# Idle products at norm ends, high halves first in the first units, and a convolution term on ScalarE in an 18-stage block stack

## The reference

```
h = rmsnorm(x, pre_g)
x = x + 0.5 * rmsnorm((silu(h @ w_gate) * (h @ w_up)) @ w_down, post_g)   # feed-forward, RMS
x = x + rmsnorm(mixer(rmsnorm(x, pre_g)), post_g)                          # mixer, RMS
x = layer_norm(ALPHA * x + f(x), g, b)                                     # the four LayerNorm stages
causal_dwconv(u, w, b): out[t] = b + sum over r in 0..3 of w[r] * u[t - 3 + r]   # per channel, 2048 channels
```

## Time and profile before

| what | us |
|---|---|
| median of 3 runs (lowest, highest) | 3450.58 (3449.51, 3451.14) |
| the profiled execution's own time | 3452.58 |
| its span, first to last instruction | 3450.8 |
| TensorE busy | 3232.1 (94%) |
| VectorE busy | 1790.2 (52%) |
| ScalarE busy | 1507.1 (44%) |
| GpSimd busy | 909.6 (26%) |
| mean granted clock of TensorE | 0.941 |

### The profile page before, as it was taken

One profiled execution on the slowest core, in us unless ns is written; L12 is line 12 of the kernel. 1 busy time (PEld: TensorE's weight loads), 2 busy tenths in 40 slices (PEclk: granted clock), 3 DMA queues, 4 the chain that ended last, 5 costly groups with the idle time before them and its releaser, 6 DMA issues.

```text
span 3450.8 us, 63449 instructions
## 1 busy us (share of the span) xinstructions
PE 3232.1 (94%) x27080; PEld 3094.7 (90%) x27080; DVE 1790.2 (52%) x3034; ACT 1507.1 (44%) x2512; POOL 909.6 (26%) x486
## 2 busy tenths in 40 slices
PE   8998999998797999988988999999899999999998
PEld 8997999996687999988977899999889999986998
DVE  5446555547664545347575444454535436445543
ACT  5444444543323444446554544344424435443442
POOL 3221232322343332322211223232213222221222
PEclk9988999998898999999998999999899999997899
DMA  6542354554101554533432435455323544540353
GB/s 228 187 160 74 129 186 163 187 174 153 68 3 50 196 186 166 186 135 117 152 116 98 147 129 186 139 172 177 102 78 131 175 168 144 169 143 25 127 173 116
DMA packets 133384, 484.49 MB, mean 140 GB/s; under 512 B 14959, under 2 KB 17151, under 8 KB 132399
## 3 DMA queue, kind: packets, MB, share of 16 engines
q1 hardware_dynamic: 131120, 470.25, 39.9%
q0 software_dynamic: 1984, 10.19, 0.9%
HBM read 479.34 MB, written 1.05 MB: 139 GB/s over the span
## 4 chain that ended last, share of the span: by engine, by line
PE 83%; DVE 8%; ACT 4%; issue 3%; POOL 1%; DMA 0%; SPq 0%; DVEq 0%; POOLq 0%; ACTq 0%
PE ps L182 82%; ACT hi L179 1%; ACT arena L179 1%; DVE lo L159 1%; PE ps L190 1%; DVE tmp L167 1%; DVE arena L159 1%; DVE arena L167 1%; DVE yT L167 1%; ACT L179 1%; POOL small L159 1%; DVE small L176 0%; DVE tmp L164 0%; DVE xT L159 0%; POOL arena L159 0%
## 5 line engine op out<-in xcount | busy, mean ns | idle before, releaser
L182 PE MATMUL ps<-hh,lo 128*128 128x256 f32 (+1 forms) x4624 | 1335.3, 289 | 0.0
L182 PE MATMUL ps<-hh,hi 128*128 128x256 f32 (+1 forms) x4336 | 1264.8, 292 | 60.0 <-DVE hl L167 26.8
L182 PE MATMUL ps<-hl,hi 128*128 128x256 f32 (+1 forms) x4336 | 1253.4, 289 | 0.0
L159 POOL TENSOR_TENSOR lo<-raw,hi 128x1024 fp32r<-128x1024 f32 x271 | 688.6, 2541 | 1827.9 <-ACT hi L179 1827.8
L179 ACT ACTIVATE hi<-raw 128x1024 fp32r<-128x1024 f32 x814 | 852.1, 1051 | 446.4 <-PE ps L182 339.7
L159 DVE TENSOR_TENSOR lo<-raw,hi 128x1024 fp32r<-128x1024 f32 x543 | 696.0, 1285 | 551.2 <-ACT hi L179 530.5
L182 PEld LDWEIGHTS ps<-hh,hi 128*128 128x128 f32 x4336 | 842.8, 194 | 73.5 <-DVE hl L167 29.5
L182 PEld LDWEIGHTS ps<-hh,lo 128*128 128x128 f32 x4624 | 896.6, 194 | 0.0
L182 PEld LDWEIGHTS ps<-hl,hi 128*128 128x128 f32 x4336 | 840.7, 194 | 0.2
L182 PE MATMUL ps<-hfh,lo 128*128 128x256 f32 (+1 forms) x1760 | 499.1, 284 | 0.0
L182 PE MATMUL ps<-hfh,hi 128*128 128x256 f32 (+1 forms) x1520 | 430.8, 283 | 0.0
(11 more groups left out here) (363 smaller groups left out, 3766.0 us busy)
## 6 DMA issues: line engine op xcount, KB each, us to landing
raw<-in_l_ffn_w_gate SPq DMA_DIRECT2D x88, 512.0 KB, 3.6
raw<-in_l_ffn_w_up SPq DMA_DIRECT2D x88, 512.0 KB, 3.7
raw<-in_l_ffn_w_down SPq DMA_DIRECT2D x88, 512.0 KB, 3.3
raw<-in_g SPq DMA_DIRECT2D x88, 512.0 KB, 3.2
raw<-in_u SPq DMA_DIRECT2D x88, 512.0 KB, 3.2
raw<-in_d SPq DMA_DIRECT2D x88, 512.0 KB, 3.2
raw<-in_ffn_w_gate SPq DMA_DIRECT2D x44, 512.0 KB, 3.2
raw<-in_ffn_w_up SPq DMA_DIRECT2D x44, 512.0 KB, 3.3
```

The source lines that it names most:

```text
L159: return self.e.tensor_tensor(o, a, b, op)
L182: return self.e.matmul(o, a, b, start=first, stop=final, skip_group_check=loose)
```

## The change

A method `hold(pe, bank, n)` issues n products of the constant identity with itself, 128 by 128 by 128, into bank 3, whose content nobody reads. They are put into TensorE's list at the three kinds of norm ends, in front of its waits. The first units of four mixers and of the feed-forward blocks (but for the first block and the one behind `Shared`) run, for each tile, the eight products with its high part after `hh(k)`, and the four with its low part after `hl(k)`. In the convolution ScalarE makes tmp = w3 * u + b out of the bank, with scale and bias from the parameter columns, ahead of its copy; VectorE is left with three steps, and only the last two wait for VectorE's own.

```diff
+    def hold(self, pe, bank, n):
+        for _ in range(n):
+            pe.mm(self.ps[bank][:, 0:P], self.ident, self.ident)
...
     def pe(self, pe):                                   # RmsExit
-        self.norm.sums(pe, [(4, self.pr(2)), (6, self.ysq(6)), (7, self.ysq(7))], False, True)
+        K, more = self.K, self.T == T3
+        self.norm.sums(pe, [(4, self.pr(2))], False, False)
+        K.hold(pe, 3, 1)
+        self.norm.sums(pe, [(6, self.ysq(6)), (7, self.ysq(7))], False, True)
+        K.hold(pe, 3, 6 if more else 4)
         self.norm.spread(pe)
+        K.hold(pe, 3, 5)
...
     def pe(self, pe):                                   # LayerExit
+        K = self.K
         self.means(pe)
-        self.norm.sums(pe, self.squares())
+        K.hold(pe, 3, 7)
+        for part, first, final, n in ((0, True, False, 2), (1, False, False, 2), (2, False, False, 1), (3, False, False, 0),
+                                      (4, False, True, 4)):
+            self.norm.sums(pe, self.squares()[part:part + 1], first, final)
+            K.hold(pe, 3, n)
         self.norm.spread(pe)
+        K.hold(pe, 3, 6)
...
     def pe(self, pe):                                   # Full
-        self.norm.sums(pe, [(k, self.sq(k)) for k in range(8)])
+        for k in range(8):
+            self.norm.sums(pe, [(k, self.sq(k))], k == 0, k == 7)
+            self.K.hold(pe, 3, 4 if k == 7 else 2 if self.T == T1 else 1)
         self.norm.spread(pe)
+        self.K.hold(pe, 3, 4)
...
+    def firsts(self, pe, u, banks):                     # Ffn; Mixer.first is changed to the same order
+        K, T = self.K, self.T
+        for k in range(8):
+            pe.wait_ge(*self.entry.hh(k))
+            for i, bank in enumerate(banks):
+                K.W.need(pe, u + i)
+                hi, lo = K.W.col(u + i, k)
+                pe.mm(bank[:, 0:T], hi, K.H[:, k, 0:T], k == 0, False)
+                pe.mm(bank[:, 0:T], lo, K.H[:, k, 0:T], False, False)
+            pe.wait_ge(*self.entry.hl(k))
+            for i, bank in enumerate(banks):
+                t = pe.mm(bank[:, 0:T], K.W.col(u + i, k)[0], K.L[:, k, 0:T], False, k == 7)
+                if k == 7:
+                    t.then_inc(K.W.done, 1)
...
                         if j > 3:                       # Hybrid.act
                             act.wait_ge(*self.cv(j - 4))
+                        act.act(K.tmp[:, j % 4, 0:T1], p, ACT.Identity, scale=K.col("conv_w_2", 48 + j),
+                                bias=K.col("conv_b_2", j))
                         t = act.act(self.uu[:, j % 4, 3:259], p, ACT.Copy)
...
-        wc = [K.col("conv_w_2", r * 16 + j) for r in range(4)]      # Hybrid.conv
-        if j > 3:
-            dve.wait_ge(*self.sx(j - 4))
-        dve.mark(dve.ts(v, u[:, 3:259], wc[3], K.col("conv_b_2", j), ALU.mult, ALU.add))
+        wc = [K.col("conv_w_2", r * 16 + j) for r in range(3)]
         for r in (2, 1):
-            dve.turn()
+            if r == 1:
+                dve.turn()
             dve.mark(dve.stt(v, u[:, r:r + T1], wc[r], v, ALU.mult, ALU.add))
```

More of the change, by code:

```diff
@@ L941, in pe @@
         start = lead or self.lazy and self.entry.start
-        for i, k in itertools.product(range(4), range(8)) if start else [(i, k) for k in range(8) for i in range(4)]:
+        if not start:
+            self.firsts(pe, self.u, K.ps[0:4])
+        for i, k in itertools.product(range(4 * bool(start)), range(8)):
             pe.wait_ge(*self.entry.hl(k))
@@ L1084, in lin, with first @@
         t.then_inc(W.done, 1)
-    def first(self, pe, u, banks, src, T, ready):
+    def first(self, pe, u, banks, src, T, high, low):
         W = self.K.W
         for k in range(8):
-            pe.wait_ge(*ready(k))
+            pe.wait_ge(*high(k))
             for i, bank in enumerate(banks):
                 W.need(pe, u + i)
-                t = pe.mm3(bank[:, 0:T], W.col(u + i, k), [x[:, k, 0:T] for x in src], k == 0, k == 7)
+                for j, w in enumerate(W.col(u + i, k)):
+                    pe.mm(bank[:, 0:T], w, src[0][:, k, 0:T], k == j == 0, False)
+            pe.wait_ge(*low(k))
+            for i, bank in enumerate(banks):
+                t = pe.mm(bank[:, 0:T], W.col(u + i, k)[0], src[1][:, k, 0:T], False, k == 7)
                 if k == 7:
@@ L1149, in pe @@
         self.entry.pe(pe)
-        self.first(pe, self.u, ps[0:4], src, T1, self.entry.hl)
+        self.first(pe, self.u, ps[0:4], src, T1, self.entry.hh, self.entry.hl)
         wg = p3(self.pg.view(), 8)
@@ L2308, in pe @@
         K, W, ps, ev = self.K, self.K.W, self.K.ps, self.ev
-        self.first(pe, self.u, ps[0:4], K.HL, T1, self.entry.hl)
+        self.first(pe, self.u, ps[0:4], K.HL, T1, self.entry.hh, self.entry.hl)
         tw, kw = [p3(self.pt.view(i), 8) for i in range(2)]
@@ L3315, in pe @@
         self.entry.pe(pe)
-        self.first(pe, self.u, ps[0:2], K.HL, T, self.entry.hl)
+        self.first(pe, self.u, ps[0:2], K.HL, T, self.entry.hh, self.entry.hl)
         wl, wg = p3(self.pl.view(0), 8), self.pl.view(1)
@@ L3863, in pe @@
         K, ps, T = self.K, self.K.ps, T3
-        self.first(pe, self.u, ps[0:4], K.HL, T, self.entry.hl)
+        self.first(pe, self.u, ps[0:4], K.HL, T, self.entry.hh, self.entry.hl)
         self.entry.norm.sums(pe, [(2 * i, self.entry.pr(i)) for i in range(4)])
```

## The result

The changed kernel takes 3415.99 us (median of 4 runs, 3413.64 to 3419.12), the kernel before 3450.05 (4 runs beside it, 3448.95 to 3451.14): ratio 0.9901, 95% interval 0.9886 to 0.9917, so 34 us or 1% faster. The forecast was 3408.4 and the range 3396 to 3430. The profiled execution took 3415.94 us, with a span of 3414.1 and a mean granted clock of 0.960, where it was 0.941.

The account below looks back on a forecast made before the run. TensorE, busy 94% of the span, was taken as the bound, so only its waits and half-clock time could be won. Terms summed to 42.2 us, taking the median to 3408.4 us, range 3396 to 3430.

Parts of the forecast that it names:

- A: Six RMS norm ends with first units behind them: 8.4 us won at three with 256 columns, 10.4 at three with 272.
- The 272-column ends: Three RMS norm ends: each to take 20.9 us, against 23.7, 24.9 and 24.4 before; 10.4 us won together.
- the end before `Shared`: RMS norm end with unchanged order: 18 half-clock products at 0.11 us each and a spread, less 0.2; 2.0 us won.
- Gla: Full norm before Gla: clock expected to fall in the sums, half the tiles at 1.5 us; 1.0 us won (-3 to 3).
- the third rival: Convolution on ScalarE: Identity needs another table, two loads per unit, 29 us lost, 3441 us; chance 0.03.
- term D: LayerNorm ends: faster sums, spreads and following products win 4.6 us before Hybrid, 3.9 at Mem's end, 2.4 at Enter3.
- E: Convolution in Hybrid: VectorE loses a step of 0.45 us per unit, ScalarE gains an Identity; 3.7 us won (0 to 6).
- Rival 2: Gain given back later: stretches paced by others, late weights, clock falling at new places; half goes, 3429 us; chance 0.13.
- term D at Mem's end: LayerNorm end at 2013: 3.9 us won, of which the sums win 0.3 only.
- term D at Enter3: Last stage's entry: VectorE waits 1.06 us a tile for ScalarE, so only the tail shortens; 1.7 + 0.7, 2.4 us won.
- Rwkv and Nsa: Full norms before these mixers: 1.1 us won before Rwkv, where VectorE mixes long after the spread, and 2.9 before Nsa.
- the first (VectorE and ScalarE pace the units): At the first units, these engines rather than TensorE set the pace; some 9 us lost, 3417 us; chance 0.13.

Follow-up runs that it names:

- keys between: Changed kernel with Hybrid's eight key products put one by one between its 16 narrow token products instead of behind them: 3416.15 us.
- no LayerNorm ones: Changed kernel without the idle products of its three LayerNorm ends, all others kept: 3418.46 us.
- meta early: Changed kernel with the meta tokens' transfer issued at the start of GpSimd's part of the LayerNorm end before: 3412.46 us.
- five: Changed kernel with sums of y and keys interleaved, more idle products in Gla's norm sums and at LayerNorm ends, early meta-token transfer: 3412.66 us.
- Gla's sums: Changed kernel with two idle products instead of one behind each tile of Gla's norm sums: 3412.51 us.
- three: Changed kernel with sums of y between Hybrid's wide products, two idle products a tile in Gla's norm sums, early meta-token transfer: 3404.96 us.

## Why the prediction was right, and where not

**Right: the mechanism and its size at the RMS ends.** A's steps can be laid beside the trace: spread at 2.66 (forecast 2.66), first high part 4.94 (4.8), end of the products 16.35 (16.1), VectorE's pairs done at 17.35 (17.3), last sums done 18.2 (17.8), so 2.4 where the term had 2.8. The last part of that term had the wrong engine last: TensorE's own sums (sixteen instructions) run without a wait from 16.35 on and take 1.84 us, as they did before, so VectorE's pairs bound nothing. The 272-column ends were forecast at 20.9 and took 20.9, 20.9 and 21.1. Of the three parts, the holds won 21 us, the order 7, the convolution 0 to 6 by what stands beside it; the sum had some 27 for the clock and 15 for the rest. So the kind of the gain was right, and a fifth of its size was missing (34 us of 42.2).

**The working.** An idle product was priced rightly (a tile in the norm before Nsa takes 0.89 us, forecast 0.90), but not because width doesn't matter: the sixteen instructions of 256 columns for the means take 3.62 us at full clock, 0.22 each and not 0.106. Some terms don't follow from their parts: the end before `Shared` comes to 2.4 by its own numbers and not 2.0, each of the first two LayerExits to 0.15 less than stated, the 272-column ends to 10.3. Together this changes nothing.

**Right: Gla, for the reason given.** The clock was expected to fall in its sums, a tile then to cost 1.5: it cost 1.51 (2428.36 to the next at 2429.87), in the last three tiles, with 0.9 us for the whole of Gla where the term had 1.0. That the number fits so well is luck: in the three other traces with the same queue in Gla (keys moved, no LayerNorm ones, early transfer) the clock falls in these sums too, but the stage came out 2.7 to 3.2 us shorter than before.

**Right: no table load.** 44 before and 44 after, at 1283 ns, so the third rival was out. By the Trainium skill ("ScalarE: Activation LUTs", Table sets) identity is in every set, and the trace agrees. The Identity with two pointers takes 0.56 us (0.6 forecast).

**Wrong: term D with E behind it, in Hybrid.** The step "23 half-clock products (2.2 us)" came true at first: from the first product of the means to the first token product 24.1 us, where 28.3 stood. The convolution also gave its part: from the fifth unit to the 17th 45.3 instead of 49.9, 4.6 us against 3.7 forecast. What failed is that I took the stage behind as given. In the sixteen narrow token products (32 instructions) the clock fell, and the keys behind them took 2.8 us more than before; up to the fifth unit 3.8 us were lost in all. Later the clock fell behind the sums of y, which it hadn't before: 1.5 us more there, and 0.4 on the way to them. Both were places that happened to be spared in the trace of the kernel before. The sums of y show this in experiments: with the convolution's edit alone 4.2 us were won and most of them lost again at the sums, and they were got back once the sums were laid between wide products. Rival 2 named this (new places where the clock falls) and sized it at half of all; here it was some 6 us (3.8, 0.4 and 1.5).

**Wrong: term D at Mem's end.** 3.9 forecast, 2.5 measured, and in truth 2.1: the sums, which were to win 0.3, cost 0.5 more than before, and this stands in the row above. The last eight sums went at 1.71 and the spread behind them at 1.06, so the clock had fallen between the idle products. The same queue of idle products had held it at 1484; why it didn't here stays open. One more of them behind the third and the fourth group was tried only as one of five edits, and in that trace too the spread took 1.06.

**Wrong: term D at Enter3.** I took VectorE's wait for ScalarE in every tile for the only bound. The start of it was a transfer, issued behind the power and landed 2.1 to 2.2 us later, which the view of all engines shows in both kernels (VectorE waited 2.81 us for it before, 2.91 after). A faster spread could win nothing there. The Trainium skill ("DMA: Bandwidth & Descriptors", Anatomy of one DMA) gives a transfer that GpSimd issues a fixed part of about 2 us, beside the time for its bytes. The 2.18 us from 2204.84 to 2207.02, for 64 KB, agree.

**Not to be credited: Rwkv and Nsa.** Rwkv's 4.3 against 1.1 made good 3 of the 10 us that were missing elsewhere, and that is luck. The last section shows that this stage scatters by more than that, and Nsa's by more still, so its 3.3 for 2.9 bears nothing out either.

Of the rivals the first (VectorE and ScalarE pace the units) found nothing in the RMS ends: TensorE's 96 products follow each other at 0.118 us.

## What to carry to other kernels

A wait that costs TensorE its clock costs the wait and the slow products behind it: look for the stretch of 0.21 us products, and fill the hole with products of 128 columns, not of one. Narrow products of the kernel's own can go between wide ones instead of in a block; for the one-column sums of y this paid, for the token products no gain was seen. And count an expected gain only up to the next thin stretch; read there too which engine or transfer is ready last before booking it.

## What the runs showed of the hardware

**The same code takes up to 7 us more or less in one stage from one trace to the next.** Windows over Nsa (first row) and Rwkv (second) of the kernel before, then of the kernel with the sums of y moved, whose code up to Hybrid is the same:

```profile
216.50:382.80 166.30, 150.99 (x1136) 137.13 (x1136) 85.79 (x189) 72.82 (x165) 25.65 (x13) 0.89 0.28 95
788.90:965.60 176.70, 146.98 (x1431) 117.34 (x1433) 126.84 (x202) 59.18 (x106) 47.67 (x38) 0.86 0.26 90
```

```profile
215.60:379.60 164.00, 148.91 (x1136) 134.52 (x1136) 86.15 (x189) 72.71 (x165) 26.23 (x12) 0.90 0.28 96
785.50:959.50 174.00, 144.30 (x1435) 115.58 (x1437) 126.95 (x202) 59.20 (x106) 47.74 (x39) 0.88 0.27 92
```

2.3 and 2.7 us apart, and the granted clock with it. Wider still are the seven traces of kernels whose code up to the end of Rwkv is the changed kernel's, as times in us between the same two powers:

| stage | changed | keys between | Gla's sums | no LayerNorm ones | meta early | five | three |
|---|---|---|---|---|---|---|---|
| Nsa | 163.4 | 162.7 | 162.5 | 157.3 | 163.5 | 160.4 | 164.3 |
| Rwkv | 172.9 | 176.2 | 176.4 | 175.9 | 172.9 | 175.9 | 171.9 |

Each is another program behind that point, and one execution; the runs of one and the same program scatter as widely. So a gain of 3 us that a single pair of profiles shows in such a stage is no finding, and as the runs of all but one of these kernels scatter by 4 to 13 us, a median of four or five tells little under 4 us apart. What is said here of smaller edits rests on the rows at their place.

**A float32 product of one column is priced by the clock too:** 0.21 us an instruction at half clock (the starts of the groups of four above are 0.86 apart), 0.11 to 0.12 at full. So the 32 sums before Nsa (6.99 us) were paced by TensorE itself; I had put that down to ScalarE's squares. The tile with two idle products came out at the 0.90 forecast all the same, since at full clock sums and idle products together take as long as the sums did at half.
